# One feed-forward chunk of both sequence halves as seven block products

## What is computed

```python
def channel_mixer(x, g_norm, w1, w2):
    h = rms_norm(x, g_norm)
    return x + jnp.square(jax.nn.relu(h @ w1)) @ w2

for layer in range(2):
    # layer 0: sparse attention (top 256 of the causal keys for each query, by an
    #   indexer's scores) beside a spatial gating unit, then one output projection
    # layer 1: pointwise conv + GLU, causal depthwise conv of width 31, RMSNorm,
    #   swish, pointwise conv
    x = even_layer(x, ...) if layer == 0 else odd_layer(x, ...)
    x = channel_mixer(x, ff_g_norm[layer], ff_w1[layer], ff_w2[layer])
```

## Time and profile before

| | |
|---|---|
| median of 3 runs | 2081.86 us (2080.52 to 2084.3) |
| span of the profiled execution | 2078.6 us |
| PE busy | 2049.6 us (99%) |
| VectorE busy | 1493.3 us (72%) |
| ScalarE, GpSimd busy | 940.3 us, 938.2 us (45% each) |
| mean DMA rate | 107 GB/s |

### The profile page before, as it was taken

The page is one execution under the profiler, slowest core; times in us unless marked ns, Lnnn a source line. Parts: engine busy times, 40 slices in busy tenths (PEclk is TensorE's granted clock), DMA queues, the critical chain, the costliest instruction groups (busy, mean ns, idle before and its releaser), DMA issues.

```text
span 2078.6 us, 29271 instructions
## 1 busy us (share of the span) xinstructions
PE 2049.6 (99%) x9690; PEld 1715.7 (83%) x9690; DVE 1493.3 (72%) x2216; ACT 940.3 (45%) x1390; POOL 938.2 (45%) x595
## 2 busy tenths in 40 slices
PE   7999899999999999999999999999999999999999
PEld 7788788888888898888888888888878888888887
DVE  6698758888888443257777634889954587979877
ACT  6644665232323663343323245444365346464562
POOL 5865674554655003556556456857664700000000
PEclk9999999999999999999999999999999999999999
DMA  6321122332323012223233222333353453434433
GB/s 213 93 70 62 45 69 81 104 95 96 102 92 101 11 54 81 92 82 111 92 102 93 100 92 91 103 101 132 122 177 106 162 205 119 162 131 141 148 128 122
DMA packets 77281, 222.62 MB, mean 107 GB/s; under 512 B 7520, under 2 KB 7904, under 8 KB 76128
## 3 DMA queue, kind: packets, MB, share of 16 engines
q1 hardware_dynamic: 73552, 214.60, 31.4%
q10 hardware_dynamic: 3600, 6.32, 0.8%
HBM read 208.31 MB, written 12.58 MB: 106 GB/s over the span
## 4 chain that ended last, share of the span: by engine, by line
PE 87%; DVE 2%; issue 1%; ACT 1%; POOL 0%; DMA 0%; ACTq 0%; DVEq 0%; POOLq 0%
PE psum L916 20%; PE psum L918 20%; PE psum L917 20%; PE psum L1267 6%; PE psum L1266 6%; PE psum L1265 6%; PE psum L1091 3%; PE psum L941 2%; PE psum L1067 1%; PE psum L1068 1%; DVE psum L2443 1%; PE psum L998 0%; POOL w_buf L1291 0%; DMA raw<-weights 0%; PE psum L1008 0%
## 5 line engine op out<-in xcount | busy, mean ns | idle before, releaser
L1291 POOL TENSOR_TENSOR w_buf<-raw,w_buf 128x1024 fp32r<-128x1024 f32 x250 | 607.5, 2431 | 459.8 <-ACT w_buf L1631 438.4
L1631 ACT ACTIVATE w_buf<-raw 128x1024 fp32r<-128x1024 f32 x236 | 248.5, 1054 | 325.7 <-PE psum L918 264.8
L916 PE MATMUL psum<-hid_buf,w_buf 128*128 128x512 f32 x896 | 350.1, 391 | 0.0
L918 PE MATMUL psum<-hid_buf,w_buf 128*128 128x512 f32 x896 | 349.3, 390 | 0.0
L917 PE MATMUL psum<-hid_buf,w_buf 128*128 128x512 f32 x896 | 349.3, 390 | 0.0
L918 PE MATMUL psum<-h_buf,w_buf 128*128 128x512 f32 x896 | 349.1, 390 | 0.0
L916 PE MATMUL psum<-h_buf,w_buf 128*128 128x512 f32 x896 | 349.1, 390 | 0.0
L917 PE MATMUL psum<-h_buf,w_buf 128*128 128x512 f32 x896 | 349.1, 390 | 0.0
L2443 DVE SCALAR_TENSOR_TENSOR psum<-y_buf,wdw,psum 128x512 f32<-128x512 f32 x435 | 295.0, 748 | 0.0
L1265 PE MATMUL psum<-hid_buf,w_buf 128*128 128x512 f32 x576 | 224.4, 390 | 0.0
L1266 PE MATMUL psum<-hid_buf,w_buf 128*128 128x512 f32 x576 | 224.4, 390 | 0.0
(11 more groups left out here) (318 smaller groups left out, 3350.4 us busy)
## 6 DMA issues: line engine op xcount, KB each, us to landing
raw<-weights SPq DMA_DIRECT2D x312, 512.0 KB, 3.5
w_more<-weights SPq DMA_DIRECT2D x48, 512.0 KB, 4.3
xt<-x_t SPq DMA_DIRECT2D x2, 2048.0 KB, 8.4
out_t<-xt SPq DMA_DIRECT2D x16, 256.0 KB, 2.0
x_in<-x_t SPq DMA_DIRECT2D x12, 256.0 KB, 6.6
m_kept<-m_ring ACTq DMA_DIRECT2D x12, 256.0 KB, 2.0
c_kept<-c_ring ACTq DMA_DIRECT2D x12, 256.0 KB, 2.7
m_in<-m_kept SPq DMA_DIRECT2D x3, 1024.0 KB, 7.1
```

The lines of the kernel that those rows point to most:

```text
L916: nc.tensor.matmul(acc, lhs_hi, rhs_hi, start=first, stop=False)
L918: return nc.tensor.matmul(acc, lhs_lo, rhs_hi, start=False, stop=last)
L1291: nc.gpsimd.tensor_tensor(dst_lo, src, dst_hi.bitcast(F32), ALU.subtract).then_inc(done, 1)
L1631: nc.scalar.activation(w_buf[:, 0, :, slot * P:(slot + 1) * P], raw[:, slot % 2], ACT.Copy).then_inc(hi_up, 1)
```

## The change

Chunk 3 of ff0 is taken out of both halves (`SOLO0 = 3` chunks stay) and is done for both at once, in a first session of block products between wout of half 1 and pw1 of half 0. Both stages of this pair (up and down) take all seven products; the six stages of the later session stay as they were.

What follows from it: the input of half 0 is kept in DRAM (`x_early`) before ff0 adds to it and comes back as `h_first` at wout of half 1; the input of half 1 is kept likewise for its ff0 after pw1. The row norm of half 1 is now needed ahead of the third product. The input of pw1 for half 0 is prepared in the last 14 steps of the session. The 64 rounds of top-k on tile pairs are re-cut into 32 on tiles 4 and 5, 21 on 6 and 7, 11 on tile 6, spread over 46 units by width, and the last 22 steps of tile 7 go behind the masks of attention slots 35 to 54. The convolution of half 0 begins in pw1 of half 0 (49 taps) and ends two units into the last chunk of ff0.

```diff
-          ("ff0", 1, FF0, 64), ("pw1", 1, PW1, 16),
+STAGES = [("wout", 0, WOUT, 8), ("ff0", 0, FF0, 16 * SOLO0), ("wout", 1, WOUT, 8), ("pw1", 0, PW1, 16),
+          ("ff0", 1, FF0, 16 * SOLO0), ("pw1", 1, PW1, 16),
...
+ROUNDS_67 = 21
+LATE_GROUPS = [(4, 5)] * ROUNDS + [(6, 7)] * ROUNDS_67 + [(6,)] * (ROUNDS - ROUNDS_67)
+LATE_SLOTS = {**{a: 1 for a in range(35, 55) if a not in (42, 50)}, 36: 2, 45: 2, 53: 2, 54: 2}
+def late_groups_at(u, end):
+    cost = [sum(t + 1.5 for t in tiles) for tiles in LATE_GROUPS]
+    at = [sum(cost[:n + 1]) * end / sum(cost) for n in range(len(cost))]
+    return [tiles for tiles, when in zip(LATE_GROUPS, at) if u < when <= u + 1]
...
+PAIRS = [(FF0, q) for q in range(SOLO0, 4)] + [(FF1, q) for q in range(SOLO, 4)]
+EARLY_PAIRS = 4 - SOLO0
+PRODUCTS = [(n, term) for n in range(PAIRED_STAGES) for term in range(TERMS)
+            if n % 2 or n < 2 * EARLY_PAIRS or term not in (A11, A12)]
+SESSION = [0, START[2 * EARLY_PAIRS], 4 * len(PRODUCTS)]
...
-PW1_TAPS = [0] * 4 + [4] * 4 + [6] * 8
+PW1_TAPS = ([0] * 5 + [3] * 3 + [5] * 8, [0] * 4 + [4] * 4 + [6] * 8)
+FF0_TAPS = [6] * 16 * (SOLO0 - 1) + [4, 3] + [0] * 14
...
 # SyncE
+                if (name, half) == ("ff0", 0):
+                    stream(first, first_block, 0, 8)
+                    sp.wait_ge(unit_read, first)
+                    sp.dma_start(x_early[0][:], xt0[:]).then_inc(x_early_saved[0], 16)
+                    stream(first, first_block, 8, count)
...
+                    sp.wait_ge(qk_masked, 64)
+                    sp.wait_ge(x_early_saved[0], 16)
+                    sp.dma_start(h_first[:], x_early[0][:]).then_inc(h_first_in, 16)
                     stream(first, first_block, 4, count)
+                    pair_loads(0)
...
 # PE
+            def pair_products(session):
+                for g in range(SESSION[session], SESSION[session + 1]):
+                    v, term, p = g // 4, term_of(g), g % 4
+                    if g == 2:
+                        mean_of("ff0_1", sum_lo)
+                    pe.wait_ge(w_lo, g // 2 + 1)
...
+                    for j in range(4):
+                        if p == 0 and j % 2 == 0:
+                            pe.wait_ge(b_lo, 2 * v + j // 2 + 1)
...
 # GpSimd, wout of half 1
+                    units(first, 8, last=True)
+                    for m in range(3):
+                        first_low_weights(m)
+                    for z in range(2):
+                        first_low_activations(1, z)
+                    first_low_weights(3)
...
 # ScalarE, wout of half 1
-                    act.wait_ge(unit_read, first)
-                    units(first, 8, again(0, "pw1_0", G_OD, h_buf))
+                    units(first, 8, both(square_second(first), keep_second(G_FF0), split_first), last=True, unrolled=True)
+                    pair_splits(0)
...
 # VectorE, wout of half 1
-                    units(first, 8, add_residual(first, half), final(0, "pw1_0", G_OD, h_buf))
+                    for m in range(8):
+                        residual(m // 4, m % 4)
+                        if m:
+                            add_squares(n0 + m - 1, (m - 1) % 2, psum[:, 7, :])
+                        if m == 2:
+                            dve.wait_ge(h_first_in, 16)
+                        if 2 <= m < 6:
+                            normalise_first(2 * m - 4, G_FF0, rms_bc)
+                            normalise_first(2 * m - 3, G_FF0, rms_bc)
+                        if m >= 6:
+                            low_activations(0, m - 6)
+                    add_squares(n0 + 7, 1, psum[:, 7, :])
+                    pair_sums(0)
...
+            def pair_sums(session):
+                first, end = SESSION[session], SESSION[session + 1]
+                if session == 0:
+                    split_sums("ff0_1")
+                    norm_of("ff0_1", rms_second)
+                    for k in range(4):
+                        normalise_second(k, rms_second)
+                for g in range(first, end):
+                    v, p = g // 4 + 1, g % 4
+                    if session == 0 and g in (5, 6):
+                        normalise_second(2 * g - 6, rms_second)
+                        normalise_second(2 * g - 5, rms_second)
...
 # VectorE, ff0 of half 0
+                            if r < 8:
+                                relu_scaled(r // 4, r % 4)
+                            else:
+                                residual((r - 8) // 4, r % 4)
+                            for tiles in late_groups_at(u, 16 * SOLO0 - 2):
+                                late_topk(2 * len(tiles))
+                            if u == 16 * SOLO0 - 2:
+                                mask(4)
+                                attention_slot(32, 1)
```

More of the change, by code:

```diff
@@ L730, in before_in_bank @@
             upper = term_of(g) in (A12, S1, S4)
-            return max((4 * v + g % 4 for v in range(g // 4) if (PRODUCTS[v][1] in (A12, S1, S4)) == upper), default=None)
+            first = SESSION[session_of(g)] // 4
+            return max((4 * v + g % 4 for v in range(first, g // 4) if (PRODUCTS[v][1] in (A12, S1, S4)) == upper),
+                       default=None)
         def w_rows(g):
@@ L882, in _ @@
             m1_load(0)
[L883 to L902 removed]
+            pair_loads(1)
             last = START[-1]
@@ L1182, in mlp @@
                     if q == 0:
-                        units(first, 8, operand, prep_lo, KT * PREP[name], mean=(name, sum_lo))
+                        units(first, 8, operand, prep_lo, KT * PREP[name],
+                              mean=None if (stage, half) == ("ff0", 1) else (name, sum_lo))
                     else:
@@ L1194, in mlp @@
                     mean = None
-                    if q == 3 and (stage, half) == ("ff0", 1):
+                    if q == chunks_of(stage)[-1] and (stage, half) == ("ff0", 1):
                         mean = ("conv0", sum_lo)
@@ L1922, in mlp @@
                         continue
-                    if q == 3 and (stage, half) == ("ff0", 1):
+                    if q == chunks_of(stage)[-1] and (stage, half) == ("ff0", 1):
                         squares = conv_squares(0)
-                    units(first + 16 * q, 8, both(hidden_hi, squares), mean=None if q else name_of(stage, half))
+                    units(first + 16 * q, 8, both(hidden_hi, squares), unrolled=squares is not None,
+                          mean=None if q or (stage, half) == ("ff0", 1) else name_of(stage, half))
                     if (stage, half) == ("ff1", 1):
@@ L2618, in mlp @@
                         continue
-                    if conv and not late and q < 3:
+                    if (stage, half) == ("ff0", 0):
+                        residual = add_residual(down, half)
                         for r in range(16):
-                            done = 16 * q + r
+                            u = 16 * q + r
+                            if u == 16 * SOLO0 - 8:
+                                split_queries(4)
                             if r < 8:
```

618 lines of the change are left out of this document (373 added, 245 removed).

## The result

The changed kernel takes 2097.73 us (median of 4 runs, 2096.06 to 2098.93), the kernel before 2081.88: 1.0077 times as long, 95% interval 1.0065 to 1.0089. That is slower by 0.77%; the forecast was 2083.4, the range ended at 2091. The profiled executions span 2094.3 and 2078.6 us: +15.7 where the sum said +1.5.

What follows compares the result with a forecast made beforehand. TensorE, busy 2049.6 of 2078.6 us, was taken as the bound; -21.8 + 8.6 + 8.5 + 5.7 + 0.5 = +1.5 us gave span 2080.1, and 3.3 for the runs' median 2083.4; range 2073 to 2091.

Steps and rivals of the forecast that it cites:

- the price of the waits: Each new TensorE wait costs its length; lower clock charged only behind the session-start wait, 1.7 us.
- edits at nothing: Weight loads queued behind copies of x, and the session's end, taken as covered: 0, up to 2 us each.
- Matmuls, -21.8: TensorE, ff0's fourth chunk in both halves: 96 fewer matmuls at 0.2267 us each, 21.8 us less.
- Top-k in 48 units, 8.6: ff0, half 0: VectorE's top-k in 48 units stalls TensorE at chunk ends and attention's start, 8.6 us (3 to 12).
- Attention, 0: Attention slots: one or two top-k steps fit the 5 us before TensorE's transpose; 0, at most 1 us.
- Session's start, 6.8: First product waits until T + 6.8 for preparation ordered behind wout's last unit; bounds 5.5 and 8 us.
- its half clock, 1.7: Behind the session-start wait TensorE restarts at the lower clock, 1.7 us more.
- Third product, T + 36.2 for its second half: VectorE readies its operand at T + 36.2, TensorE arrives at T + 30.5: gap 5.7 us, bounds 3.4 and 9.
- T: Signal of the last unit of wout, half 1, from which the session-start times are counted.
- The end of the session: Last 14 steps, 38 us, hold 33 us of VectorE work; taken as covered, up to 2 us if not.
- Pointwise one, 0.5: pw1: VectorE with convolution steps ends 1.3 us late with 1.3 of cover: 0.5 us, up to 3.
- Rival 2: Half clock behind three shorter gaps too, 5.1 us more, 2088.5; chance 0.32 together with another slower rival.

Runs made afterwards that it cites:

- the reordered kernel: Changed kernel with session start reordered, early inputs later, input split ahead of sigmoid, top-k groups held back at two chunk ends: 2075.52 us, 0.9970 of before.
- experiments 8 and 11: 8: changed kernel, top-k groups held back past two chunk ends, 2088.87 us; 11: reordered kernel, every fourth late top-k group on 16 columns, 2073.83 us.
- experiment 7: Changed kernel with ff0's late top-k groups (half 0) spread over 44 units instead of 46: 2098.58 us, 1.0082 of before.
- experiment 1: Changed kernel with idle-filling matmuls in TensorE's waits, 26 ahead of the session's first product and 12 ahead of the third: 2098.34 us, 1.0082 of before.
- experiment 6: Changed kernel with four of pw1's early inputs later and convolution taps moved off pw1's last two units: 2094.15 us, 1.0058 of before.
- second run of experiment 6: Changed kernel with ScalarE's split of ff0's input ahead of the gate's sigmoid in pw1, half 0: 2093.01 us, 1.0054 of before.
- experiment 3: Changed kernel with the third product's first weight sum on VectorE moved ahead of the norm: 2094.49 us, 1.0059 of before.
- experiment 4: Changed kernel with the first product's preparation on ScalarE and VectorE moved ahead of the last wout unit's work: 2094.80 us, 1.0057 of before.
- experiment 9: Changed kernel with session start reordered, early inputs and taps moved, and top-k spread over 44 units: 2087.24 us, 1.0025 of before.
- experiment 5: Changed kernel with the whole session start reordered: first product's preparation, mean, root, sums and normalisations: 2089.95 us, 1.0041 of before.

## Why the prediction was wrong

The forecast was no change; the kernel became slower by 0.77%. The step that failed is the price of the waits: half clock was charged behind one of them and put at nothing behind the others, where it measured 9.4 us. The second is "edits at nothing", two waits mis-sized by 4.1 us together. The bullets follow the terms of the sum.

- **Matmuls, -21.8:** the count is right. No run shows the price by itself; the reordered kernel, with some waits and half clocks left, is 6 us faster than before.
- **Top-k in 48 units, 8.6:** near in each place: 3.3, 1.9, 0.9 and 2.5 were forecast, 2.91, 1.90, 0.63 and 3.64 measured, the last above its 1 to 3.2. What it took for a lack of time is mostly order (experiments 8 and 11).
- **Attention, 0:** mis-sized by 1.4. The 5 us of slack were read from the earlier trace rows, which are of a later tile. The wait of 1.37 us at 621.91 stands in all thirteen profiles with the change, also in experiment 7's (1.36), where the first slot isn't late, so lateness doesn't cause it. VectorE works on top-k of tile 7 just ahead of it (615.2 to 621.6); no run takes that away, and the cause stays open.
- **Session's start, 6.8, and its half clock, 1.7:** right, with 6.64 and 2.1 measured.
- **Third product, T + 36.2 for its second half:** the time of the chain was right to a tenth (36.2). In the changed kernel two errors cancel in it: the norm is ready at T + 17.9, not T + 16.1, as PE's mean comes late under the half clock, and the scalings take 3.2 us, not 4.8. With the clock up (experiment 1) both are near the forecast, 15.9 and 5.05. That the sum was right with the half clock too is luck. The gap was not right: 5.7 against 3.5, because PE was put there at full speed while its half clock had been charged beside it. The 1.7 stood in the sum twice, which experiment 1 shows: the half clock ahead of that wait cost nothing.
- **Edits at nothing:** this step failed. "The end of the session" had 33 us of VectorE's work in 38, and was held to be covered. The sum was right (34.1 us busy from 891 to 931), its spread was not: in the 16 us up to the wait at 907 VectorE is busy for 15.96. Four early inputs stand ahead of the low halves of the last product but one (2.2 us, experiment 6). **Pointwise one, 0.5:** the wait for ScalarE's split in every second unit was put down (1.6 us, 1.31 measured), but VectorE ended 4 us late, not 1.3, and the wait was 2.4. Its main cause is the sigmoid ahead of the split (second run of experiment 6).
- **The clock:** the largest failure, 9.4 of the 13.4 us between forecast and account. The forecast charged one gap, on the ground that the only row was one of 7.58 us. Rival 2 had the mechanism, three places and a start from about 3 us; there were five, two of them behind 2.2 and 2.4 us. It gave 2088.5, and 2097.7 was measured. The page it named, the Trainium skill, "TensorE: Matmul & The Clock Gate", section "Part 1: The HAM clock gate", speaks of half rate behind idle time; the traces agree (granted 0.52 to 0.62 in the six windows behind waits), and experiment 1 ties it to the idle time for the longest of them. That no such row was there for a shorter wait was taken as half an argument against; it was none.

## What to carry to other kernels

A wait of 1.4 to 4 us on TensorE can have two prices here, its length and up to 3 us of half clock behind it. The second is not always paid: what the full clock would give can be lost again ahead of the next hand-over, as it was here to GpSimd. Where a change takes TensorE work from above an engine that is 85% busy, look not at that engine's sum but at the last operation ahead of each hand-over, and put what isn't due behind it. One order of independent steps was worth 22 us here, as much as the removed work.

## What the runs showed of the hardware

- The price of a gap isn't fixed. The same wait of 2.91 us at the first chunk's end was followed by half clock at a cost of 1.7 us in the changed kernel and 3.0 in experiment 1, and by none in experiments 3 and 4; the wait of 1.90 us by none in the changed kernel and by 1.6 in experiment 4. Shorter waits can have it too: behind the 1.37 us in attention, seven of the thirteen profiles show half clock, six don't. Windows over these places, from experiment 1; experiment 3; experiment 4 (both waits); and experiment 9, behind the 1.37 us:

```profile
385.10:391.20 6.10, 6.10 (x15) 4.81 (x16) 4.78 (x9) 1.06 (x1) 4.65 (x2) 0.51 0.28 86
```

```profile
385.00:389.00 4.00, 3.95 (x17) 3.30 (x18) 3.37 (x6) 1.06 (x1) 4.00 (x2) 1.00 0.12 14
```

```profile
387.00:391.00 4.00, 3.92 (x17) 3.28 (x18) 3.37 (x6) 1.06 (x1) 4.00 (x3) 1.00 0.12 18
478.00:482.00 4.00, 4.00 (x13) 3.15 (x12) 4.00 (x7) 0.47 (x1) 2.95 (x2) 0.60 0.43 131
```

```profile
622.50:626.00 3.50, 3.46 (x15) 3.27 (x16) 1.02 (x3) 1.23 (x3) 0.00 (x0) 0.52 0.00 0
```

  Single executions of one kernel differ by as much. Of the ten of the reordered one, the two fastest (2072.7 and 2073.1 us) have a mean granted clock of 1.000, the two slowest (both 2078.2) of 0.997 and 0.998. What decides it in a given execution stays open.
- Two SBUF inputs on VectorE beside GpSimd: four scalings of 128x512 in 3.17 us beside little of GpSimd's work, 4.70 (experiment 5) and 5.05 (experiment 1) beside more of it, a 128x1024 sum 1.21 alone and 2.17 beside it (changed kernel and experiment 5).
